# Attention scored keys by queries, with the row maxima in a 97th row of q, in a fused two-block fp32 kernel

## The reference

```
def causal_block_attention(q, k, v):        # q, k: 8 heads x 96, v: 8 heads x 64, L = 1040
    ...
        s = jnp.einsum('bqhd,bkhd->bhqk', q[:, q0:kend], k[:, :kend]).astype(jnp.float32) * scale
        ...
        s = jnp.where(valid, s, MASK_VALUE)
        p = jax.nn.softmax(s, axis=-1).astype(v.dtype)
        outs.append(jnp.einsum('bhqk,bkhd->bqhd', p, v[:, :kend]))
```

## Time and profile before

| What | Value |
|---|---|
| runs | 3590.38, 3588.11, 3587.58 us; median 3588.11 |
| profiled execution, span | 3590.0 us |
| TensorE busy | 3411.0 us, 95% |
| VectorE / ScalarE / GpSimd busy | 1925.4 / 1442.7 / 221.1 us |
| layer 0: q/k stage from 1777.7, attention from 1895.2, stage 4 from 2137.0 | us from the span's start |
| layer 1: q/k stage from 2768.6, attention from 2886.1, stage 4 from 3130.8 | us from the span's start |

### The profile page before, as it was taken

How to read it: one execution, slowest core, us unless ns; L and a number is a source line. 1 busy time by engine, 2 the same in 40 slices (tenths; PEclk the granted TensorE clock), 3 DMA queues, 4 the chain that set the end, 5 groups by cost and what they waited for, 6 DMA issues and landing times.

```text
span 3590.0 us, 49054 instructions
## 1 busy us (share of the span) xinstructions
PE 3411.0 (95%) x19515; PEld 2787.4 (78%) x19515; DVE 1925.4 (54%) x2710; ACT 1442.7 (40%) x2189; POOL 221.1 (6%) x225
## 2 busy tenths in 40 slices
PE   6799877899999999999999999999999999999998
PEld 6577555777778877889856779999998567787887
DVE  6767588756444444446654544444546645444433
ACT  4442465444332333234344443333343444433322
POOL 1000033210000000000020000000000200000000
PEclk7999988889999999999999999999999999999999
DMA  6444101023333324323200102343432001023333
GB/s 235 157 149 161 47 24 60 7 94 133 97 112 118 94 94 165 94 94 114 79 1 13 42 25 86 115 139 89 142 123 79 1 13 42 24 85 112 122 92 112
DMA packets 94595, 321.56 MB, mean 90 GB/s; under 512 B 10320, under 2 KB 11616, under 8 KB 93600
## 3 DMA queue, kind: packets, MB, share of 16 engines
q1 hardware_dynamic: 75392, 246.52, 21.4%
q0 software_dynamic: 17440, 67.65, 5.4%
q10 hardware_dynamic: 1536, 4.26, 0.3%
HBM read 295.26 MB, written 23.20 MB: 89 GB/s over the span
## 4 chain that ended last, share of the span: by engine, by line
PE 78%; DVE 12%; ACT 6%; issue 1%; DMA 1%; DVEq 0%; POOL 0%; ACTq 0%; SPq 0%; POOLq 0%
PE psum L146 75%; DVE mixer L171 4%; PE psum L149 3%; DVE mixer L181 2%; DVE wlo L171 1%; DVE junk L185 1%; DVE arena L171 1%; ACT arena L155 1%; DVE arena L194 1%; DMA stage<-in_wm 1%; ACT whi L163 1%; DVE region L171 1%; ACT L155 1%; DVE mixer L198 0%; ACT mixer L154 0%
## 5 line engine op out<-in xcount | busy, mean ns | idle before, releaser
L146 PE MATMUL psum<-region,whi 128*128 128x260 f32 (+2 forms) x7616 | 1834.0, 334 | 6.4 <-DVE region L181 3.2
L146 PEld LDWEIGHTS psum<-region,whi 128*128 128x128 f32 (+1 forms) x7616 | 1278.7, 186 | 173.5 <-DVE region L171 9.6
L146 PE MATMUL psum<-region,wlo 128*128 128x260 f32 (+2 forms) x3808 | 1265.7, 332 | 0.0
L171 DVE TENSOR_TENSOR wlo<-stage,whi 128x1024 fp32r<-128x1024 f32 (+2 forms) x454 | 512.7, 1129 | 654.4 <-ACT whi L163 618.8
L146 PEld LDWEIGHTS psum<-region,wlo 128*128 128x128 f32 (+1 forms) x3808 | 711.2, 187 | 78.4
L163 ACT CAST whi<-stage 128x1024 fp32r<-128x1024 f32 (+2 forms) x454 | 441.9, 973 | 251.7 <-PE psum L146 163.1
L146 PE MATMUL psum<-arena 128*128 128x65 f32 (+8 forms) x2064 | 400.4, 341 | 4.1 <-ACT arena L155 2.3
L163 ACT COPY arena<-psum 128x512 f32<-128x512 f32 (+10 forms) x428 | 190.4, 445 | 403.4 <-PE psum L146 359.5
L154 ACT ACTIVATE arena<-psum 128x260 f32<-128x260 f32 (+1 forms) x188 | 92.4, 492 | 574.3 <-PE psum L146 574.2
L146 PEld LDWEIGHTS psum<-arena 128*128 128x128 f32 (+4 forms) x2064 | 246.1, 175 | 95.1 <-issue 84.9
L171 DVE TENSOR_TENSOR arena<-arena 128x512 f32<-128x512 f32 (+8 forms) x324 | 202.8, 626 | 153.7 <-ACT arena L154 142.7
(11 more groups left out here) (148 smaller groups left out, 3024.0 us busy)
## 6 DMA issues: line engine op xcount, KB each, us to landing
stage<-in_w SPq DMA_DIRECT2D x144, 512.0 KB, 3.5
stage<-in_wi SPq DMA_DIRECT2D x55, 512.0 KB, 4.4
stage<-in_wo SPq DMA_DIRECT2D x48, 512.0 KB, 3.6
stage<-in_wg SPq DMA_DIRECT2D x44, 512.0 KB, 3.6
stage<-in_wu SPq DMA_DIRECT2D x44, 512.0 KB, 3.6
stage<-in_wm SPq DMA_DIRECT2D x42, 512.0 KB, 3.6
stage<-in_wd SPq DMA_DIRECT2D x32, 512.0 KB, 3.5
arena<-xr_scratch POOLq DMA_DIRECT2D x5, 2080.0 KB, 10.6
```

Of the source, the lines that this page charges most:

```text
L146: return Issued(self, self.e and self.e.matmul(out, w, x, start=start, stop=stop, skip_group_check=True))
L171: return Issued(self, e and e.tensor_tensor(out, a, b, op))
```

## The change

Scores are formed keys by queries, so that exp of them can be the moving operand of the value product. The row maximum, which must then be subtracted along the free dimension, comes from a product of its own, in one fp32r pass, in the old orientation (128 queries by all their keys, in 14 pieces a head, `PIECES`); its negation is turned to a row and copied by a GpSimd DMA into row 96 of q, where row 96 of k is 1, so that the score product of 97 rows subtracts it. P is neither turned nor copied. The value product has [V | ones] (64 + 64 columns) as stationary operand and up to 512 queries as moving one, so that its other 64 rows are the sums of P, repeated; two copies bring outputs and sums to `oT` and `rs`, and a reciprocal and a multiplication over 512 columns normalise two heads at a time. `HEADS` is 4 to 7, then 0 to 3. Two casts (`act_round`, 1,024 and 1,040 columns) round a head's q and k for it. The maxima of head n + 1 are formed between the tiles of head n (`AT`); those of head 0 in the q/k stage. The 16 meta queries are done apart, in layer 0 alone. All `pe_fill` of the attention go, the one at t = 8 stays.

```diff
-        m.vv = ar[:, 0:NTB * 520].rearrange("p (t h x) -> p t h x", h=8, x=65)
+        m.vx = ar[:, 0:NTB * 768].rearrange("p (t a x) -> p t a x", a=4, x=192)
+        m.qx, m.kx = m.cqk[0:97], [v(k, 4, L2)[0:97] for k in m.kr]
+        m.q1 = [whi[:, 2304:3328], art[0:96, 1848:2872]]
+        m.k1 = [wlo[:, 2304:2304 + L2], arr[1][0:96, free - U:free - U + L2]]
+    TILES = []
+    for ch, q0 in enumerate((NM, NM + 512)):
+        for c in range(5 if ch == 0 else 9):
+            qs = max(q0, c * 128)
+            TILES.append((ch, c, qs, q0 + 512 - qs, min(128, q0 + 512 - c * 128)))
+    PER = len(TILES)
+    for i in range(8):
+        J = 128 * i + 144
+        nb = (J + 511) // 512
+        cut_ = [J * j // nb // 8 * 8 for j in range(nb + 1)]
+        PIECES += [(i, j, cut_[j], cut_[j + 1], j == nb - 1) for j in range(nb)]
+    AT = [(0, 2), (2, 4), (4, 5), (5, 7), (7, 8), (8, 10), (10, 11), (11, 13), (13, 14)] + 5 * [(14, 14)]
+    FIRST = [[p for p, x in enumerate(PIECES) if x[0] == i] for i in range(8)]
+    SPLIT_AT = {PER * n + 4: n - 1 for n in range(2, 6)}
+    MAX_BANKS, KEY_BANKS, OUT_BANKS, ONE_BANK, PG_BANKS = (0, 1), (2, 3, 4), (5, 6), (7,), (6, 7)
+    def beside_heads(bs, g):
+        if g >= 5 * PER and g % 2 == 0:
+            bs.tick()
+    def pe_max(e, l, n, p, among):
...
+        ins = e.matmul(psum[:, b, 0:w], m.q1[n > 0][:, 128 * i:128 * i + 128], m.k1[n > 0][:, k0:k1], True, not last)
+        if last:
+            ins = e.matmul(psum[:, b, w - 128:w], IDB, NEGS, False, True)
+    def pe_scores(e, l, g):
...
+        if c == 0:
+            e.wait_ge(*rowd[ch][l, n])
...
+        ins = e.matmul(psum[0:w, b, 0:nq], m.kx[h // 4][:, h % 4, c * 128:c * 128 + w], m.qx[:, h, qs:qs + nq], True, not masked)
+        if masked:
+            ins = e.matmul(psum[0:w, b, 0:w - d], IDB[:, 0:w], NEGT[:, d:w], False, True)
+    def pe_values(e, l, g):
...
+        e.wait_ge(*A["e", g])
+        e.matmul(psum[:, b, 512 - nq:512], m.vx[0:w, c, h // 2, x0:x0 + 128], m.pt[0:w, g % 5, 0:nq], c == 0,
+                 c == 4 * ch + 4).then_inc(*T.up("pv", g))
     def pe_att(e, bs, l):
...
+                if t >= 2:
+                    if t < 8:
+                        e.wait_ge(*A["xT", t - 1, 3])
+                        for p in FIRST[t - 2]:
+                            pe_max(e, l, 0, p, range(8))
+                    else:
+                        pe_row(e, l, 0, 0)
+                        pe_fill(e, bank, psum, C, 10)
...
+        for p in FIRST[6] + FIRST[7]:
+            pe_max(e, l, 0, p, range(8))
+        for g in range(NG + 2):
+            n, k = divmod(g, PER)
+            beside_heads(bs, g)
+            if g < NG:
+                pe_scores(e, l, g)
+            if g >= 2:
+                pe_values(e, l, g - 2)
+            if g < 2:
+                pe_pg(e, l, (2 + g,))
+            if g == 2:
+                pe_row(e, l, 0, 1)
+            if n < 7:
+                for p in range(*AT[k]):
+                    pe_max(e, l, n + 1, p, MAX_BANKS)
+                if k in (4, 10):
+                    pe_row(e, l, n + 1, k // 10)
+            if l == 0 and n == 1:
+                pe_meta(e, l, k)
     def act_att(e, bs, l):
...
+        act_round(e, l, 1, "q")
+        act_round(e, l, 1, "k")
         act_pg(e, l, (0, 1))
...
+                e.activation(m.pt[0:w, g % 5, 0:nq], psum[0:w, bank.of["s", l, g], 0:nq], ACT.Exp).then_inc(*A.up("e", g))
...
+            if n < 7 and k in (5, 11):
+                act_row(e, l, n + 1, k // 11)
+            if n < 6 and k in (9, 10):
+                act_round(e, l, n + 2, "qk"[k - 9])
+            if g >= 3 and (g - 3) % PER in (4, PER - 1):
+                act_out_of(e, l, (g - 3) // PER, (g - 3) % PER // (PER - 1))
     def dve_att(e, bs, l):
...
+            if 3 <= t < 9:
+                dve_max(e, l, 0, FIRST[t - 3])
...
+        dve_max(e, l, 0, FIRST[6] + FIRST[7])
+            if n < 7:
+                dve_max(e, l, n + 1, range(*AT[k]))
+            if k == 9 and n:
+                dve_share(e, l, (n - 1) // 2, (n + 1) % 2)
...
+        dve_share(e, l, 3, 1)
     def pool_att(e, bs, l):
...
-        e.memset(m.vv[:, :, :, 64:65], 1.0).then_inc(*G.up("ones", l))
+        e.memset(m.vx[:, :, :, 64:128], 1.0).then_inc(*G.up())
+        for x in m.ones:
+            e.memset(x, 1.0).then_inc(*G.up())
...
+        for n in range(8):
+            for c in range(2):
+                e.wait_ge(*A["row", n, c])
+                e.dma_start(m.qx[96:97, HEADS[n], NM + 512 * c:NM + 512 * c + 512], m.row[:, c, :]).then_inc(
+                    *rowd[c].up(l, n, by=16))
+            if n == 4:
+                bs.flush()
```

More of the change, by code:

```diff
@@ L2674, in act_pg @@
                              scale=P[f"ps_{l}"][:, g:g + 1]).then_inc(*A.up("pg", g, c))
+    def pe_max(e, l, n, p, among):
+        S, m = slay[l], M[l]
+        T, A, D = S.pe, S.act, S.dve
+        i, j, k0, k1, last = PIECES[p]
+        w = k1 - k0
+        if n and p == 0:
+            e.wait_ge(*A["rounded", n])
+        b, free = bank.take(("mx", l, n, p), D, "mx", n, p, among=among)
+        for f in free:
+            e.wait_ge(*f)
+        ins = e.matmul(psum[:, b, 0:w], m.q1[n > 0][:, 128 * i:128 * i + 128], m.k1[n > 0][:, k0:k1], True, not last)
+        if last:
+            ins = e.matmul(psum[:, b, w - 128:w], IDB, NEGS, False, True)
+        ins.then_inc(*T.up("mx", n, p))
@@ L2688, in pe_att @@
                     if t == 0:
[L2689 removed]
+                        e.wait_ge(*wkd[g][l])
                         for half in range(2):
@@ L2782, in pe_att, with act_round, act_row @@
         bs.flush()
         T.mark("att", l)
+    def act_round(e, l, n, what):
+        S, m = slay[l], M[l]
+        T, A, D = S.pe, S.act, S.dve
+        h = HEADS[n]
+        if n >= 2:
+            e.wait_ge(*T["mx", n - 1, len(PIECES) - 1])
+        if what == "q":
+            e.copy(m.q1[1], m.qT[:, h, NM:L2]).then_inc(*A.up())
+        else:
+            e.copy(m.k1[1], m.kT[h // 4][:, h % 4, :]).then_inc(*A.up("rounded", n))
+    def act_row(e, l, n, c):
+        S, m = slay[l], M[l]
+        T, A, D = S.pe, S.act, S.dve
+        e.wait_ge(*T["row", n, c])
+        if n:
+            e.wait_ge(*rowd[c][l, n - 1])
+        e.copy(m.row[:, c, :], psum[0:4, bank.of["row", l, n, c], 0:128]).then_inc(*A.up("row", n, c))
@@ new lines, in act_att, with dve_max @@
+        bs.flush()
+    def dve_max(e, l, n, pieces):
+        S, m = slay[l], M[l]
+        T, A, D = S.pe, S.act, S.dve
+        for p in pieces:
+            i, j, k0, k1, last = PIECES[p]
+            e.wait_ge(*T["mx", n, p])
+            e.tensor_reduce(m.pmx[:, i, j:j + 1], psum[:, bank.of["mx", l, n, p], 0:k1 - k0], ALU.max).then_inc(
+                *D.up("mx", n, p))
+            if last and i in (3, 7):
+                c = i // 4
+                if n:
+                    e.wait_ge(*T["row", n - 1, c])
+                e.tensor_reduce(m.nm[:, 4 * c:4 * c + 4], m.pmx[:, 4 * c:4 * c + 4, :], ALU.max, negate=True).then_inc(
+                    *D.up("nm", n, c))
@@ L2864, in dve_att, with dve_share @@
+    def dve_share(e, l, pr, ch):
+        S, m = slay[l], M[l]
+        T, A, D = S.pe, S.act, S.dve
+        o = m.oT[:, HEADS[2 * pr] // 2, NM + 512 * ch:NM + 512 * ch + 512]
+        e.wait_ge(*A["out", 2 * pr + 1, ch])
+        e.reciprocal(m.rs[:, ch, :], m.rs[:, ch, :]).then_inc(*D.up())
+        e.tensor_tensor(o, o, m.rs[:, ch, :], ALU.mult).then_inc(*D.up("norm", pr, ch))
     def dve_att(e, bs, l):
```

307 lines of the change are left out of this document (156 added, 151 removed).

## The result

Median 3486.45 us of four runs (3483.50 to 3488.71) beside 3588.39 for the kernel before (four runs): ratio 0.9715, 95% interval 0.9701 to 0.9729, faster by 102 us. The forecast was 3465, with a range of 3440 to 3505. The profiled execution took 3487.83 us with a span of 3486.0; against the span of 3590.0 that is -104.0 where the sum had -123.3.

A forecast was written before the change was run, and what follows sets the result against it. TensorE was taken to bound the attention. Layer 0 -60.1, layer 1 -67.4 and q/k stages +4.2 gave -123.3 on the span of 3590.0: 3466.7, stated as 3465 us, range 3440 to 3505.

The forecast's parts named there:

- The rival of four passes: Maxima products in all heads and q/k stages run in four passes, not one: +90 us, 3555; chance 0.02.
- the rival of VectorE's order: In the attention, VectorE's order delays TensorE, 2.5 us a head instead of 0.7: +25, 3490; chance 0.17.
- signs of being wrong: TensorE idle before maxima pieces or a half's first tile, clock under 1 after the start, waits for exp at short tiles.
- The head: New attention head on TensorE: scores 8.24, values 8.24, maxima 2.16, masks 1.08, row turns 0.22; sum 19.9 us.
- Masks: 10 + 8 at 0.06: Mask products of one attention head on TensorE, each delaying its successor by 0.06 us: 1.08 us a head.
- Two tiles of 16 columns at 0.2: The two 16-column tiles among a head's scores, 0.2 us each within 8.24; values costed at the same 8.24.
- +0.7 stalls: TensorE stalls from instruction order in the attention: 0.7 us a head, bounds 0 and 2.5, making 20.6 a head.
- a stall of 0 to 2.5, I take 1.5: TensorE's wait for the DMA of the row that releases head 0's second half: 1.5 us a layer.
- Layer 1's q/k stage: Maxima 1.3, masks 0.4 and the last tile's chain 0.4 added to each layer's q/k stage: +2.1 us.
- clock 2.5 us: Allowance for lower granted clock after waits at the attention's start: 2.5 us a layer.
- The start: From the q/k stage to the first score, after ScalarE's copies, casts and pooling activations: 6.9 us a layer.
- the dummies go (2.6): Dummy products of the old attention head counted as TensorE work that the change removes: 2.6 us a head.

The follow-up runs named there:

- the last three versions: Changed kernel with row turn behind dummies, pooling activations first, six more dummies: 3481.43 us; also head 1's casts on GpSimd: 3472.72; also three pooling banks: 3472.59.

## Why the prediction was right, and where its sum was off

**Right.** The sign, the mechanism and the range; TensorE bounds the attention and nothing of VectorE, ScalarE or the DMAs shows in an ordinary head. The reciprocal at tile 9, the casts and rows of later heads, GpSimd's memsets and stage 4's load were costed at nothing and cost TensorE nothing. Layer 0's q/k stage took 1.5 more for 2.1. The rival of four passes was priced at +90 and measures +87 (3573.66 to 3486.45).

**In part luck.** The result lies near the 3490 at which the rival of VectorE's order was priced, and that rival did not come: the upper half of the range had been left for a stall on VectorE, and was used up by TensorE's own products, which no rival named. The meta queries' 4.8 for 4.4 is luck too: 3.3 of products and 1.5 of clock. Of the signs of being wrong that the forecast named one came, a granted clock under 1 after the start (at 1942). The chances that it gave to itself and its rivals add up to 0.99.

**The head: 19.9 of work forecast, 21.78 found** (20.6 with the stalls). This is the term that was sized wrongly and carries most of the miss.
- "Masks: 10 + 8 at 0.06" was read from the earlier trace rows as the distance from a mask to its successor. What it does to the successor was left out: the product behind begins on time and then lasts some 0.055 longer. 18 masks at 0.11 instead of 0.06: +0.9. The Trainium skill, in TensorE: Matmul & The Clock Gate, section "LDWEIGHTS (loading the stationary operand)", gives the columns divided by 1.2 as nanoseconds for a weight load, 107 for 128 columns. 0.053 and 0.055 together agree with it.
- "Two tiles of 16 columns at 0.2": with their neighbours' bared loads the 16-row value tiles cost some 0.5 each (0.43 by the starts at 3011.60 and 3012.48, and 0.09 on the product ahead). +0.6.
- The maxima cost 3.3 a head for 2.86: a head without them takes 18.4 by the two halves of the last head (5.7 and 12.7), one with them 21.8 (7.5 and 14.2). The extra is that of their eight masks, counted in the first item.
- The passes run at 0.431 for 512 columns and not 0.427: +0.2. The rest, some 0.1, is not assigned to one thing.
- Against that, "+0.7 stalls" was 0: only the head with a split and scalings stalls, 0.67 once a layer.

The forecast had said itself that a record does not fall under 0.11 us, and did not apply this to masks. Over some eight heads a layer, 1.2 us a head is 9 to 10 us a layer. It is partly given back by the row: "a stall of 0 to 2.5, I take 1.5" was 0, since the row's DMA was issued at 1913.37, such DMAs take 1.6 us from issue to landing (median of the sixteen in layer 0), and the second half's first score at 1915.39 did not wait.

**Layer 1's q/k stage: +6.8 instead of +2.1.** The work was sized rightly (layer 0 shows it). The row turn's wait for a bank was not seen: about 2.1 us, which every run with the turn ahead of the dummies pays in layer 1. The other 3.3 are the clock's fall behind it, which this run had and three others with such a wait did not; "clock 2.5 us" was placed at the start only. With the turn behind the dummies the stage is 118.9, under the forecast of 119.6.

**The start: 8.2 and 8.9 instead of 6.9.** Order and casts were as forecast (casts from 1896.58, pooling activations at 1898.75 for 1899.0). The time until the first score was short by 1.3 and 2.0. TensorE waits 3.30 us, until the first of the five pooling activations has freed a bank (1899.35), and the last pooling product starts at 1900.67, as forecast (1900.7). What was short is the rest: in both layers that product and the first maxima run at a granted clock of 0.50 (1899.35 to 1902.60 in layer 0), which the forecast did not put into this term.

**Dummies: "the dummies go (2.6)".** The old head's 29.17 was explained as work, dummies included. The run without them shows that they filled waits and held the clock. The forecast came out near, since the new head was summed from its own products and not as a difference.

## What to carry to other kernels

Price a short product not by the distance to its successor but by both neighbours: between long products a mask of 128 columns cost 0.11 us here, about as much as one of 256. Put dummy products ahead of the first instruction that can wait, not behind it (2.1 us here, and the clock in some runs), and check in every layer which bank that instruction gets. Where an orientation needs a second product of the same size, its passes decide whether it pays: one pass cost 3.3 us a head, four would have cost 9.0.

## What the runs showed of the hardware that was not expected

- TensorE's granted clock fell to 0.69 at 1942 to 1946, TensorE busy 4.00 of 4.00 us by its records, in a stretch in which the meta queries' small products stand (sixteen of the records at 1941.64). Without them it stayed at 1.00. With them it also stayed at 1.00 in the run with masks of 256 columns, so the same work can run at either clock. The forecast had looked for the clock's falls behind waits only.
- The same wait of 2.5 us in layer 1's q/k stage was followed by the lower clock in the kernel after and by the full clock in the run without the meta queries (ten dummy products: 4.03 and 2.40 us). A difference of a few us between two single runs can be this alone.
- A second mask of the same weights costs 0.052 us and thirteen masks of twice the width 0.11 together: this fits that a stream and the next weight load overlap, and that a product about as long as the load bares none of it.
- GpSimd casts 96 x 1024 from fp32 to fp32r in 1.03 us, ScalarE in 1.04.
- What stands ahead of the layers is the same in all the kernels tried, yet layer 0's q/k stage starts between 1772.2 and 1780.7 us. Totals of single runs that differ by less say nothing; the readings above rest on stretches of the trace, and on four runs each for the last three versions.
